# A whole transformer step on one core: the second norm's weights move to the experts' transposed rows, and the expert choice is split in two

## What is computed

```python
def rms_norm(x, g):
    y = xf * lax.rsqrt(jnp.mean(xf * xf, axis=-1, keepdims=True) + RMS_EPS)
    return (y * g.astype(jnp.float32)).astype(x.dtype)
...
h = h + moe_ffn(rms_norm(h, ffn_norm_g), ...)
...
g_sel = jnp.argmax(g_logits, axis=-1)            # the group of 8 experts, of 4
top_v, top_i = lax.top_k(e_in_group, TOP_K)      # 2 experts of the 8
...
hb = jax.nn.silu(xb @ w_exp_gate[e]) * (xb @ w_exp_up[e])
return (hb @ w_exp_down[e]) * wt[:, None]
```

## Time and profile before

| what | value |
|---|---|
| three executions | 1079.25, 1079.64, 1081.33 us |
| median | 1079.64 us |
| span of the profiled execution, first to last instruction | 1078.2 us |
| TensorE busy, with the clock granted over the span | 948.8 us, 0.972 |
| VectorE, ScalarE, GpSimd busy | 338.8, 201.7, 196.8 us |
| DMA over the span | 283.82 MB |

### The profile page before, as it was taken

How to read it: one execution, slowest core, us unless ns; L and a number is a source line. 1 busy time by engine, 2 the same in 40 slices (tenths; PEclk the granted TensorE clock), 3 DMA queues, 4 the chain that set the end, 5 groups by cost and what they waited for, 6 DMA issues and landing times.

```text
span 1078.2 us, 12247 instructions
## 1 busy us (share of the span) xinstructions
PE 948.8 (88%) x4745; PEld 534.2 (50%) x4745; DVE 338.8 (31%) x756; ACT 201.7 (19%) x446; POOL 196.8 (18%) x296
## 2 busy tenths in 40 slices
PE   7989999999999999999998999888888877877870
PEld 6644444777676566774553544424334243432420
DVE  3269999965441111330135000000000000000016
ACT  3143110223343334001121000000000000000012
POOL 2740650100001200000231112201111111111122
PEclk9999999999999999999999999999899999999995
DMA  9920211430203832934038999999999999999986
GB/s 341 395 97 1 78 57 68 153 149 18 79 1 138 265 145 69 359 153 156 40 131 322 423 424 422 423 419 426 423 422 424 422 426 421 425 425 423 418 341 208
DMA packets 53690, 283.82 MB, mean 263 GB/s; under 512 B 8684, under 2 KB 9552, under 8 KB 33031
## 3 DMA queue, kind: packets, MB, share of 16 engines
q1 hardware_dynamic: 42807, 246.24, 57.0%
q0 software_dynamic: 10784, 36.97, 9.4%
q10 hardware_dynamic: 56, 0.01, 0.0%
HBM read 267.41 MB, written 23.17 MB: 270 GB/s over the span
## 4 chain that ended last, share of the span: by engine, by line
PE 55%; DMA 26%; DVE 3%; ACT 2%; issue 2%; SPq 1%; POOL 0%; POOLq 0%; ACTq 0%; DVEq 0%
DMA arena<-in_w_exp_up 24%; PE psum L788 11%; PE psum L957 6%; PE psum L626 5%; PE psum L975 5%; PE psum L1063 4%; PE psum L1060 4%; PE psum L1061 4%; PE psum L1080 3%; PE psum L909 1%; DMA y_d<-arena 1%; PE psum L875 1%; PE psum L837 1%; PE psum L859 1%; PE psum L999 1%
## 5 line engine op out<-in xcount | busy, mean ns | idle before, releaser
L1063 PE MATMUL psum<-arena 128*64 128x512 f32 x704 | 164.1, 619 | 28.9 <-DMA arena<-in_w_exp_up 28.2
L1080 PE MATMUL psum<-arena 128*64 128x512 f32 x512 | 116.9, 597 | 17.7 <-ACT arena L1365 17.7
L788 PE MATMUL psum<-arena 128*128 128x288 f32 x480 | 124.6, 412 | 0.0
L1063 PEld LDWEIGHTS psum<-arena 128*64 128x64 f32 x704 | 54.8, 143 | 136.2 <-issue 101.6
L788 PEld LDWEIGHTS psum<-arena 128*128 128x128 f32 x480 | 88.4, 190 | 30.3 <-issue 8.1
L1734 DVE TENSOR_TENSOR arena<-arena,psum 128x256 f32<-128x256 f32 x32 | 13.5, 421 | 274.7 <-ACT arena L1361 274.7
L1361 ACT ACTIVATE arena<-psum 128x256 f32<-128x256 f32 x32 | 12.3, 383 | 402.8 <-PE psum L1063 270.5
L626 PE MATMUL psum<-arena 128*128 128x512 f32 x192 | 84.5, 594 | 0.2 <-ACT arena L1232 0.2
L1080 PEld LDWEIGHTS psum<-arena 128*64 128x64 f32 x512 | 40.4, 136 | 72.1 <-issue 71.4
L1060 PE MATMUL psum<-arena 128*64 128x256 f32 x320 | 56.8, 413 | 15.3 <-DMA arena<-in_w_exp_up 15.3
L1742 DVE COPY arena<-psum 128x512 f32<-128x512 f32 x31 | 21.4, 692 | 152.2 <-PE psum L1080 152.2
(11 more groups left out here) (291 smaller groups left out, 1090.0 us busy)
## 6 DMA issues: line engine op xcount, KB each, us to landing
arena<-in_w_exp_down SPq DMA_DIRECT2D x32, 2048.0 KB, 36.9
arena<-in_w_exp_gate SPq DMA_DIRECT2D x29, 2048.0 KB, 32.3
arena<-in_w_exp_up SPq DMA_DIRECT2D x19, 2048.0 KB, 37.2
arena<-in_w_exp_up SPq DMA_DIRECT2D x26, 1024.0 KB, 33.4
arena<-in_w_in SPq DMA_DIRECT2D x7, 2048.0 KB, 8.8
y_d<-arena SPq DMA_DIRECT2D x1, 8192.0 KB
arena<-in_w_exp_gate SPq DMA_DIRECT2D x6, 1024.0 KB, 13.9
arena<-in_x_prompt SPq DMA_DIRECT2D x8, 512.0 KB, 8.2
```

The lines of the kernel that those rows point to most:

```text
L788: last = pe.matmul(bank(2 + n % 2 if n < SAMPLE_G else 2, HN), ring[slot % 2][:, k, m * P:(m + 1) * P], xnT[:, k, HN * hh:HN * hh + HN], s ...
L1063: last = pe.matmul(bank(2 + s, 512, rows).rearrange("p (w n) -> p w n", w=2), x_k, wgu[j][:, :, DE * k + 256 * q:DE * k + 256 * q + 256], ...
L1080: last = pe.matmul(bank(4 + s, 512, slice(64 * half, 64 * half + 64)), hT[s][:, k % 2, CAP * (k // 2):CAP * (k // 2) + CAP], wd[j][:, k, 5 ...
```

## The change

The norm's weights leave the stored rows. ACT writes the scaled rows directly into `xn2` in the order that the store wants, and POOL only stores them. `g2row` (512 KB, for all partitions) becomes `g2cols` (8 values for each partition), and `take_x` moves from ACT to DVE, where it multiplies by them. The choice of experts becomes `choose(t0, t1)`: tiles 0 and 1 are chosen inside the output projection, tiles 2 to 4 behind it. The row numbers are taken out ahead of the six small instructions. SyncE loads the down matrix of expert 2 after the last `route` and no longer after the gather of expert 1.

```diff
-                sp.dma_start(g2row, ffn_norm_g.to_broadcast([P, D])).then_inc(S["late_in"], 16)
+                sp.dma_start(g2cols, ffn_norm_g[0].rearrange("(p k) -> p k", k=KD)).then_inc(S["late_in"], 16)
...
             sp.dma_start(flat(wu2[1]), u_v[2, :, 4 * DE:]).then_inc(s_gu[2], 16)
+            sp.wait_ge(S["r_done"], TILES)
+            load_down(2, 2)
             sp.wait_ge(M[1]["xg_in"], 16)
-            load_down(2, 2)
...
             keep_busy(7, 7, resid[:, 0, 0:512])
-            pe.wait_ge(S["a_ready"], 1)
+            pe.wait_ge(S["a_ready"], 2)
...
-                if i >= 2:
-                    act.wait_ge(S["xn2_r"], i - 1)
...
-                act.activation(xs2[i % 2][0:r, :], resid[0:r, i, :], ACT.Copy, scale=rstd2[0:r, i:i + 1]).then_inc(S["xs2_r"], 1)
+                if i >= 2:
+                    act.wait_ge(s_xst[i % 2], 16 * (i // 2))
+                act.activation(xn2[i % 2][0:r, :].rearrange("r (h p t) -> r p h t", h=2, t=4), resid[0:r, i, :].rearrange("r (p h t) -> r p h t", h=2, t=4),
+                               ACT.Copy, scale=rstd2[0:r, i:i + 1]).then_inc(S["xn2_r"], 1)
...
-            def take_x(m, s, n):
-                act.wait_ge(m["xt_done"], n + 1)
-                act.copy(xT[s].rearrange("p k t -> p (k t)"), bank(0)).then_inc(m["xt_ev"], 1)
...
+            def choose(t0, t1):
+                ts, n = slice(t0, t1), t1 - t0
...
+                first_of(gl, EG, gm, gh, a[:, :, 0:EG], b[:, :, 0:EG], low)
...
+                first_of(v, NE, best, hot1, a, b, low)
+                link(dve.scalar_tensor_tensor(v, hot1, -2 * NEG, v, ALU.mult, ALU.add))
+                first_of(v, NE, second, hot2, a, b, low)
...
+                dve.tensor_tensor(ab[:, ts, :], a, signed[:, ts, :], ALU.mult).then_inc(S["a_ready"], 1)
...
+            FIRST_TILES = 2
             add_residual(0)
             add_residual(1)
             for i in range(2, TILES):
                 take_turned(i - 2)
+                if i == TILES - 1:
+                    dve.wait_ge(S["r_add"], FIRST_TILES)
+                    choose(0, FIRST_TILES)
                 take_logits(i - 2)
...
+            choose(FIRST_TILES, TILES)
...
                 dve.tensor_tensor(sl, sl, r, ALU.add)
+                if hot is t32[3]:
+                    dve.wait_ge(S["tok_done"], 1)
+                    dve.tensor_scalar(sidx2, bank(5, 2), const("lift"), None, ALU.add).then_inc(S["tok_out"], 1)
...
                 link(dve.tensor_scalar(pmax, r, -1.0, CAP - 1.0, ALU.mult, ALU.add))
...
+            def take_x(m, s, n):
+                dve.wait_ge(m["xt_done"], n + 1)
+                dve.tensor_tensor(xT[s].rearrange("p t (h c) -> p t h c", h=2), bank(0).rearrange("p (t h c) -> p t h c", h=2, c=CAP),
+                                  g2cols.rearrange("p (h t) -> p t h", t=KD // 2).unsqueeze(3).to_broadcast([P, KD // 2, 2, CAP]),
+                                  ALU.mult).then_inc(m["xt_ev"], 1)
...
                 expert_h(m, s, n)
+                if ahead:
+                    take_x(M[1 - s], 1 - s, n + s)
                 dve.wait_ge(m["y_done"], n + 1)
...
-                pool.tensor_tensor(xn2[i % 2][0:r, :].rearrange("r (h p t) -> r p h t", h=2, t=4),
-                                   xs2[i % 2][0:r, :].rearrange("r (p h t) -> r p h t", h=2, t=4),
-                                   g2row[0:r, :].rearrange("r (p h t) -> r p h t", h=2, t=4), ALU.mult).then_inc(S["xn2_r"], 1)
```

More of the change, by code:

```diff
@@ L293, in program @@
         W2D = o
-        g2row, wr = at(W2D + D, D), at(W2D + 2 * D, KD, P); o += 4 * D
+        wr = at(W2D + 2 * D, KD, P); o += 4 * D
         assert W2D + 2 * D >= ZB and KD * P == D
@@ L307, in program @@
         pmax = at(o, TILES); o += TILES
+        g2cols = at(o, KD); o += KD
         flag = arena[:, o:o + 1].bitcast(I32); o += 1
@@ L1365, in take_h, with expert_pair @@
                 act.copy(hT[s].rearrange("p k t -> p (k t)"), bank(1, KE * CAP)).then_inc(m["ht_ev"], 1)
-            def expert_pair(i, last_pair=False):
+            def expert_pair(i):
                 for s in range(2):
                     silu(M[s], s, i)
-                    if not (last_pair and s == 1):
-                        take_x(M[1 - s], 1 - s, i + s)
                     take_h(M[s], s, i)
-            take_x(M[0], 0, 0)
             expert_pair(0)
@@ L1377, in _ @@
                 expert_pair(i)
-            expert_pair(NE // 2 - 1, True)
+            expert_pair(NE // 2 - 1)
             act.wait_ge(M[1]["y_done"], NE // 2)
@@ L1387, in _ @@
                         n = e * NB + b + N0
-                        take_x(OV, 0, n)
                         silu(OV, 0, n)
@@ L1637, in _, with first_of, over @@
             dve.wait_ge(S["late_in"], 80)
+            iota = const("iota")
+            def first_of(v, n, top, hot, a, b, low):
+                shape = [P, v.shape[1], n]
+                def over(x):
+                    return x.unsqueeze(2).to_broadcast(shape)
+                link(dve.tensor_reduce(top, v, AX, ALU.max))
+                link(dve.tensor_tensor(a, v, over(top), ALU.is_equal))
+                link(dve.scalar_tensor_tensor(b, a, -64.0, iota[:, 0:n].unsqueeze(1).to_broadcast(shape), ALU.mult, ALU.add))
+                link(dve.tensor_reduce(low, b, AX, ALU.min))
+                link(dve.tensor_tensor(hot, b, over(low), ALU.is_equal))
@@ L1712, in _ @@
             dve.tensor_copy(flag, least[:, 0:1]).then_inc(S["flag_ready"], 1)
+            def take_x(m, s, n):
[3 more added lines that the diff above has]
+                                  ALU.mult).then_inc(m["xt_ev"], 1)
+            take_x(M[0], 0, 0)
             dve.wait_ge(S["gexp_out"], 2)
@@ L1734, in expert_h, with expert @@
                 dve.tensor_tensor(hb[s], sg[s], bank(2 + s, DE // 2, at0=DE // 2), ALU.mult).then_inc(m["h_ready"], 1)
-            def expert(m, s, n, stored=None):
+            def expert(m, s, n, stored=None, ahead=True):
                 expert_h(m, s, n)
+                if ahead:
+                    take_x(M[1 - s], 1 - s, n + s)
                 dve.wait_ge(m["y_done"], n + 1)
@@ L1762, in _ @@
                 with dve.Fori(N0, N0 + NE * NB) as n:
-                    expert(OV, 0, n, 32 * n - 16 * N0)
+                    take_x(OV, 0, n)
+                    expert(OV, 0, n, 32 * n - 16 * N0, ahead=False)
                 dve.wait_ge(S["sc_st"], 16 * 3 * TILES)
```

56 lines of the change are left out of this document (22 added, 34 removed).

## The result

| | before | after |
|---|---|---|
| median of 11 runs | 1080.39 us (1079.25 to 1081.33) | 1083.61 us (1081.25 to 1085.40) |
| profiled execution: own time, span | –, 1078.2 us | 1083.86, 1082.3 us |
| first load of expert 3 issued | 585.02 | 588.95 |
| last five weight loads begin to be issued | 1019.36 | 1021.95 |

The ratio of after to before is 1.003, with a 95% interval of 1.0022 to 1.0038: the change costs 3.2 us. Forecast were 1078.9 us and a range from 1074.2 to 1082.0. The spans of the two profiled executions lie 4.1 apart.

A forecast was written before the change was run, and what follows sets the result against it. The expert stage was taken as bound by the weight stream at 423 GB/s. Expert 3's first load landing 0.7 us earlier gave span 1077.5; with the median 1.44 above, 1078.9 us, range 1074.2 to 1082.0.

The forecast's parts named there:

- The sibling of line 1658: DVE instruction in the choice of experts: 0.2 us forecast once POOL's multiply is gone, where line 1658 took 1.10.
- ACT's write in the new order: Stores of the rows: taken at the time of ACT's plain copy, with 2.35 us as upper bound.
- Rival 1: Expert 0's gather isn't held up: 4.6 us at most, end at 1074.7 or 1073.6; chance 0.3 including values between.
- turns by packet: DMA engines alternate between queues with work, a packet at a time; by this rule the unheld gather would be the outcome.
- the clock: PE at expert 0's gate_up: idle 4.3 us, then half clock for two us, 1.2 us lost; bounds nothing and about 2.
- one window of 2 us: Trace window from 714 to 716 us: granted clock 0.50 after a wait of 2.65 us, basis of the clock's price.
- own range: End time in the main case: 1077.9 to 1080.5 us with expert 0's gather at 6.6 to 9.2.
- makes it good: Expert stage: PE enters 3 us later and catches up while it waits for the stream, at no cost.
- last sign: Stream from 590 us: gaps or a rate other than 423 GB/s would prove the account by the stream's start wrong.
- account by the landing: Gain counted in expert 3's first load: landing at 592.8 against 593.5, so -0.7 us.
- exactly: Expert stage: its end moves by exactly what the start of the continuous weight stream moves.
- a gather of 10.7 us: Slower rival: expert 0's gather held like tile 3's store, 2.4 us later, 1082.0; chance 0.2 with later starvation.

The follow-up runs named there:

- run 4: Changed kernel with expert 2's down matrix issued behind expert 0's gather, ahead of expert 1's: 1079.03 us, 0.9986 of before.
- run 12: Changed kernel, early down matrix included, with the filling matmuls of run 9: 1081.94 us, 1.0015 of before.
- Run 3: Changed kernel with eight more filling matmuls on PE ahead of expert 0: 1079.50 us, 0.9993 of before.
- run 2: Kernel before with only expert 2's down matrix issued early, after the last route: 1086.00 us, 1.0054 of before.
- run 1: Changed kernel with expert 2's down matrix issued behind expert 1's gather again: 1078.89 us, 0.9995 of before.
- run 5: Kernel before with `take_x` moved from ACT to DVE as a plain copy: 1080.03 us, 1.0000 of before.
- run 6: Kernel before with only the row numbers taken out ahead of the overflow count: 1079.97 us, 0.9993 of before.
- run 8: Kernel before with two filling matmul groups behind every expert's down product but the last pair's: 1081.52 us, 1.0015 of before.
- run 10: Run 1 without the split, one `choose(0, TILES)` behind the output projection: 1078.95 us, 0.9989 of before.
- run 11: Run 9 with the last norm's weights loaded behind the four loads of expert 3: 1079.56 us, 0.9992 of before.
- run 7: Run 1 with two filling matmul groups behind every expert's down product but the last pair's: 1080.47 us, 1.0010 of before.
- run 9: Run 1 with fillers only behind the fourth and fifth expert of each round of six but the first: 1078.79 us, 0.9985 of before.

## Why the prediction was wrong

**Right, step by step.** `choose(0, 2)` ran from 548.11 to 553.3 and cost nothing: DVE still stood idle for 1.77 us ahead of the last residual. The sibling of line 1658 takes what was forecast, without GpSimd's multiply. DVE's timeline of the changed kernel:

```profile
556.61 0.68 DVE L1601 TENSOR_TENSOR arena<-psum,arena 64x512 f32<-64x512 f32 x1 [1.77 <-PE psum L973]
...
562.33 0.17 DVE L1641 TENSOR_TENSOR arena<-arena 128x12 f32<-128x12 f32 x1
...
572.12 0.22 DVE L1709 TENSOR_SCALAR arena<-psum,arena 128x2 int32<-128x2 f32 x1
```

From 1.10 to 0.17 us: of the 0.93, hardly any is the smaller size. This fits the Trainium skill, "SBUF — State Buffer", section "Who interferes with whom": VectorE and GpSimd share a pair of ports that one of them holds for a whole instruction. ACT's write in the new order took 1.15 us for the small tile, as its plain copy did before, which the sum had assumed. The ranks started when keep_busy ended (567.80), the row numbers came out at 572.12 (forecast 572.7), the gather started at 573.23 (573.8) and landed 7.32 later (7.6), at 580.55 (581.4). This trace starts 0.36 earlier at the last residual, which covers most of the rest. The down matrix went out right behind line 544. PE stood idle for 4.11 us (4.3). `take_x` was free.

**Rival 1** fell where the prediction put it: with the down matrix in the queue the gather took 7.3 us, without it 4.0 in the same kernel (5.27 in run 4, the most without it). The Trainium skill's turns by packet, as cited there, would have had it under 4.6; no run with the 2 MB ahead of the gather came below 6.8.

**The first step that failed is the clock.** The prediction put 1.2 us on it, "and about 2" as a bound. Measured: 3.0, in the first half of gate_up alone (2.0 in run 12). Two mistakes are in it. The price was taken from one window of 2 us, and the row beside it says more: its ten matmuls took 3.95 us, where ten of the 32 that take 7.09 are 2.2, a loss of 1.7. In that place the low level began behind the first matmuls (the clock from 712 to 714 reads 0.81); here all of gate_up up to 588 was at the low level, and the half takes 6.68 us for 3.68. And the bound was wrong by its own words: if all of the half gate_up falls into it, it takes twice its 3.6 us, a loss of 3.6 and not 2. With the right bound in place of the 1.2, the slow end of the own range would have been at 1080.5 + 3.6 - 1.2 = 1082.9.

**The second, and by size the larger, is "makes it good".** The load landed at 593.85 and not at 592.8, which accounts for 1.05. The prediction then held that PE, 3 us behind, catches up unseen. It doesn't at once: the stream needs buffers that PE frees, so being 3.9 us behind turns into a dip (348 GB/s from 602 to 604, 399 from 590 to 620), and the last loads begin 2.59 later, 2.2 more than the landing says. Run 3, with PE on time, moves 417 GB/s in the same 30 us, run 2, with PE 5.6 behind, 371. By the prediction's own last sign (a rate that isn't 423) its account by the landing fails, and the profiles say when. Where the first load of expert 3 still has loads ahead of it and lands 7.4 to 8.5 us after its issue (before, runs 1, 4, 5, 6, 8 and 10), the last loads begin 425.8 to 426.0 behind that landing, whatever else differs. Where the queue has run dry and it lands after 4.8 to 5.0 (after, runs 2, 3, 11 and 12), they begin 427.3 to 428.3 behind it; runs 7 and 9 (7.8 and 6.8) lie between, at 426.9 and 427.1. The forecast itself had the queue empty and the landing at 4.8, and still counted the whole gain by the landing.

**The third is "exactly".** That the end moves with the start of the stream, one for one, holds, once the dip is counted, up to the last experts only. The stage also ends later when PE's clock drops in expert 29; that is 1.7 us at GpSimd's scatters, and the prediction hadn't looked at the tail at all. The drop sits there in run 1 as well, and works against its gain. The table of terms for the profiled execution, forecast and measured: landing -0.7 and +0.35, dip 0 and +2.24, tail 0 and +1.55; sum -0.7 and +4.1.

**The sign.** Slower had a chance of 0.2, by a gather of 10.7 us "with later starvation of the stream by PE's delay". The gather kept to the forecast length, and its rival fell. The starvation came, and it had been given no price. The rival that was missing is the forecast's own case with the clock's full price and one for PE's delay.

## What to carry to other kernels

A prefetch that fills a queue early isn't free when a small dependent transfer starts behind it: put large loads behind the gather that the next stage waits for, or give the engine that waits some filling work. Price the lower clock by what whole pieces of work behind such waits took (here 8.5 to 10.1 us for 7.1), not by one short window, and take the next piece at half speed as the bound. Where the forecast leaves a queue empty, don't count by the landing of the first load: look at when its later loads can be issued. And where a stream sets the pace, follow what an engine's delay does to the last two stages, since there nothing covers it any more.

## What was not expected of the hardware

- The clock doesn't follow the length of the wait alone. Expert 0's gate_up took 7.09 us behind waits for its rows of 0.80 (run 1) and 2.07 (run 4), and 8.78 behind 0.95 and 0.82 (runs 9 and 11), in kernels that differ ahead of it in the place of one or two loads; in run 7, alike with run 9 up to there, it took 7.09 behind 0.92. The changed kernel and run 12, also alike up to there, have 10.08 and 8.71.
- Waits in the stream add up in a rhythm: in the kernel before expert 28 lost the clock behind 2.90 us (8.75 for gate_up), in the changed one it kept it behind 2.96 (7.09) and expert 29 lost it. In the nine profiles without fillers among the experts the place goes with the front: with the first load of expert 3 issued at 583.69 to 585.02 expert 28 has the loss, with an issue at 582.32 to 582.62 or 588.95 to 590.62 expert 29. That the shift is the cause is not shown.
- The spread of the runs is not explained. Fillers that hold the clock in expert 29 went with 2.0 us in run 9 (5.2 in run 1 without them), but with 4.9 in run 11 and 4.3 in run 12 (4.2 in the changed kernel).
- A gather of 0.26 MB took 6.8 to 7.3 us where 2 MB had been queued 3.6 to 4.3 us ahead of it (after, runs 2, 3, 12), and 3.2 to 5.3 where they had not.
